# Hybrid encoder layer on one core: seven-product pairs with joined high and low activations, and products chained in a bank

## The reference

```python
xn = rmsnorm(h, g_pre_mix)
proj = xn @ w_in          # q, k, v of two attentions, and gate_a, gate_b
...
mix = (jax.nn.sigmoid(gate_a) * ya + jax.nn.sigmoid(gate_b) * yb) @ w_out
h = h + rmsnorm(mix, g_post_mix)
gu = rmsnorm(h, g_pre_ffn) @ w_ffn_in
g, u = jnp.split(gu, 2, axis=-1)
h = h + rmsnorm((jax.nn.silu(g) * u) @ w_ffn_out, g_post_ffn)
e = p_l @ w_ple
h = h + rmsnorm(jax.nn.sigmoid(h @ w_ple_gate) * e, g_ple)
```

## Time and profile before

| | |
|---|---|
| median of 3 runs | 2796.68 us (2796.5 to 2797.44) |
| profiled execution: span, first to last instruction | 2793.8 us |
| PE busy | 2759.9 us (99%) |
| PEld busy | 2465.9 us (88%) |
| DVE busy | 1677.4 us (60%) |
| ACT busy | 997.8 us (36%) |
| mean granted clock of TensorE | 0.998 |

### The profile page before, as it was taken

How to read it: one execution, slowest core, us unless ns; L and a number is a source line. 1 busy time by engine, 2 the same in 40 slices (tenths; PEclk the granted TensorE clock), 3 DMA queues, 4 the chain that set the end, 5 groups by cost and what they waited for, 6 DMA issues and landing times.

```text
span 2793.8 us, 41330 instructions
## 1 busy us (share of the span) xinstructions
PE 2759.9 (99%) x16624; PEld 2465.9 (88%) x16624; DVE 1677.4 (60%) x2113; ACT 997.8 (36%) x1323; POOL 18.3 (1%) x25
## 2 busy tenths in 40 slices
PE   8999999999999999999999999999999999999997
PEld 7999888888888888878999999999998888888886
DVE  7888555555554432376888888888883233234534
ACT  7333323323334322253444444444442121113422
POOL 0000000000000000000000000000000000000000
PEclk9999999999999999999999999999999999999999
DMA  6434422222225444253433333333327352443322
GB/s 251 151 114 136 138 76 75 75 84 83 75 91 163 138 153 141 91 196 136 151 114 141 122 132 131 125 138 117 146 92 295 103 181 99 157 155 124 131 96 105
DMA packets 158298, 364.75 MB, mean 131 GB/s; under 512 B 17142, under 2 KB 51438, under 8 KB 155630
## 3 DMA queue, kind: packets, MB, share of 16 engines
q1 hardware_dynamic: 146304, 325.33, 34.1%
q10 hardware_dynamic: 11886, 37.87, 3.4%
HBM read 321.15 MB, written 42.00 MB: 130 GB/s over the span
## 4 chain that ended last, share of the span: by engine, by line
PE 87%; issue 10%; DVE 1%; ACT 1%; DMA 1%; SPq 0%; POOL 0%; DVEq 0%; POOLq 0%
PE bank L2204 10%; PE bank L2202 10%; PE bank L2203 10%; PE bank L2122 10%; PE bank L2124 10%; PE bank L2123 10%; PE bank L1948 8%; PE bank L1946 8%; PE bank L1947 8%; PE bank L1979 1%; DMA x_f<-xT 0%; DVE resid_b L1643 0%; PE bank L2271 0%; PE bank L1967 0%; ACT x_f L771 0%
## 5 line engine op out<-in xcount | busy, mean ns | idle before, releaser
L736 ACT CAST w_hi<-w_raw 128x1024 fp32r<-128x1024 f32 x290 | 292.3, 1052 | 934.6 <-PE bank L2204 522.7
L1188 DVE TENSOR_TENSOR w_lo<-w_raw,w_hi 128x1024 fp32r<-128x1024 f32 x288 | 341.0, 1222 | 454.4 <-ACT w_hi L736 454.3
L2122 PE MATMUL bank<-act_hi,w_hi 128*128 128x256 f32 x1664 | 471.2, 283 | 2.4 <-DVE act_lo L1279 1.4
L2123 PE MATMUL bank<-act_lo,w_hi 128*128 128x256 f32 x1664 | 470.9, 283 | 0.0
L2124 PE MATMUL bank<-act_hi,w_lo 128*128 128x256 f32 x1664 | 470.9, 283 | 0.0
L2122 PEld LDWEIGHTS bank<-act_hi,w_hi 128*128 128x128 f32 x1664 | 319.4, 192 | 2.9 <-DVE act_lo L1279 1.6
L2123 PEld LDWEIGHTS bank<-act_lo,w_hi 128*128 128x128 f32 x1664 | 319.5, 192 | 0.1
L2124 PEld LDWEIGHTS bank<-act_hi,w_lo 128*128 128x128 f32 x1664 | 319.5, 192 | 0.0
L1946 PE MATMUL bank<-act_hi,w_hi 128*128 128x512 f32 x752 | 299.5, 398 | 1.2 <-DVE w_lo L1188 1.2
L1947 PE MATMUL bank<-act_lo,w_hi 128*128 128x512 f32 x752 | 293.2, 390 | 0.0
L1948 PE MATMUL bank<-act_hi,w_lo 128*128 128x512 f32 x752 | 293.1, 390 | 0.0
(11 more groups left out here) (263 smaller groups left out, 5422.5 us busy)
## 6 DMA issues: line engine op xcount, KB each, us to landing
w_raw<-w_in SPq DMA_DIRECT2D x92, 512.0 KB, 4.2
w_raw<-w_ffn_out SPq DMA_DIRECT2D x88, 512.0 KB, 4.5
w_a_even<-w_ffn_in SPq DMA_DIRECT2D x80, 512.0 KB, 5.3
w_a_odd<-w_ffn_in SPq DMA_DIRECT2D x60, 512.0 KB, 4.4
hid_dram<-hid_st ACTq DMA_DIRECT2D x44, 512.0 KB, 5.2
w_raw<-w_ffn_in SPq DMA_DIRECT2D x36, 512.0 KB, 5.4
w_raw<-w_out SPq DMA_DIRECT2D x32, 512.0 KB, 4.5
w_raw<-w_ple_gate SPq DMA_DIRECT2D x32, 512.0 KB, 4.3
```

The source lines that it names most:

```text
L736: nc.scalar.copy(w_hi[:, 2 * par + half], w_raw[:, half]).then_inc(hi_ready, 1)
L1188: nc.vector.tensor_tensor(w_lo[:, 2 * par + half], w_raw[:, half], w_hi[:, 2 * par + half].bitcast(F32), ALU.subtract).then_inc(lo_ready, 1)
L2122: nc.tensor.matmul(out, w_hi[:, slot, k], hi, start=k == 0, stop=False)
L2123: nc.tensor.matmul(out, w_hi[:, slot, k], lo, start=False, stop=False)
```

## The change

Each step k of a product has two matmuls in place of three: the high weights meet the high and the low activations side by side in one matmul of 512 columns, and the low weights meet the high activations in one of 256 columns, on the first half of the same bank. A bank then holds a product in its first half and a correction (high by low) in its second, and the two have to be added. Products that belong to one output are chained in one bank, each going on where the one before stopped: products 0 and 3 in bank a, 1 and 5 in bank g, 2, 4 and 6 in bank b, which starts from a copy of bank a after product 0. Two sets of three banks alternate from pair to pair. ACT copies a bank or half of one after products 0, 1, 2, 3, 4 and 6 (`keep_chain`), and DVE makes four sums into `gu` and `up` and two sums of 512 columns before them, in place of seven. In DVE's step for product j, `combine_first` stands ahead of `product_low` and `combine_second` behind it, and the multiplications L1813 and L1819 are behind them both. `act_hi` and `act_lo` become the two halves of one tensor.

```diff
@@ -130,7 +130,10 @@
 PRODUCT_FROM = ((0, 0), (1, None), (3, 0), (0, 1), (2, 2), (4, None), (0, 3))
 SUM_AT = {1: 1, 3: 2, 4: 3, 6: 4}
-LAST_READ = (1, 5, 1, 3, 4, 6, 7)
+CHAIN_BANKS = ((0, 1, 5), (2, 3, 4))
+CHAIN_OF = (0, 1, 2, 0, 2, 1, 2)
+COPIES = 6
+SUMS = 4
 def shape_constants():
...
@@ -175,8 +178,8 @@
-        act_hi = at("act_hi", R_X, [P, KT, T], F32R)
-        act_lo = at("act_lo", R_X + 32 * KB, [P, KT, T], F32R)
+        act_both = at("act_both", R_X, [P, 2, KT, T], F32R)
+        act_hi, act_lo = act_both[:, 0], act_both[:, 1]
...
@@ -235,10 +238,8 @@
-        x_sum = at("x_sum", R_Q + 54 * KB, [P, S])
-        y_sum = at("y_sum", R_Q + 55 * KB, [P, S])
-        v_sum = at("v_sum", R_Q + 48 * KB, [P, S])
-        first_product = at("first_product", R_Q + 49 * KB, [P, S])
+        second_kept = at("second_kept", R_Q + 48 * KB, [P, 2, S])
+        third_kept = at("third_kept", R_Q + 54 * KB, [P, 2, S])
...
@@ -271,6 +272,8 @@
+        fifth_kept = at("fifth_kept", R_S + 3 * KB, [P, 2, S])
+        low_half = at("low_half", R_S + 5 * KB, [P, 2, S])
...
@@ -817,6 +821,30 @@
+            def keep_chain(p, q, j, before):
+                a, g, b = CHAIN_BANKS[q % 2]
+                if j == 0:
+                    if before > 1:
+                        act.wait_ge(combined, p * SUMS - SUMS)
+                    nc.scalar.copy(bank[:, b], bank[:, a]).then_inc(kept, 1)
+                elif j == 1:
+                    if before:
+                        act.wait_ge(combined, p * SUMS - 2)
+                    nc.scalar.copy(second_kept[:].rearrange("p a t -> p (a t)"), bank[:, g]).then_inc(kept, 1)
+                elif j == 2:
+                    if before:
+                        act.wait_ge(combined, p * SUMS - 1)
+                    nc.scalar.copy(third_kept[:].rearrange("p a t -> p (a t)"), bank[:, b]).then_inc(kept, 1)
+                elif j == 3:
+                    nc.scalar.copy(low_half[:, 0], bank[:, a, S:]).then_inc(kept, 1)
+                elif j == 4:
+                    nc.scalar.copy(fifth_kept[:].rearrange("p a t -> p (a t)"), bank[:, b]).then_inc(kept, 1)
+                elif j == 6:
+                    if before:
+                        act.wait_ge(combined, p * SUMS)
+                    nc.scalar.copy(low_half[:, 1], bank[:, b, S:]).then_inc(kept, 1)
@@ -847,8 +875,9 @@
             for p in range(GATE_PAIRS):
                 for j in range(PRODUCTS):
                     act.wait_ge(op_done, p * PRODUCTS + j + 1)
-                    if j == 0:
-                        nc.scalar.copy(first_product[:], bank[:, 0, 0:S]).then_inc(first_kept, 1)
+                    if j == 0 and p < 2:
+                        act.wait_ge(unit_read, 3 + p)
+                    keep_chain(p, p, j, p)
                     p4, j4 = p + (j + 4) // PRODUCTS, (j + 4) % PRODUCTS
                     if p4 < GATE_PAIRS:
                         product_high(p4, p4 % 4, j4, H_GATES)
@@ -1106,8 +1135,7 @@
                     f = p0 + (CH + q)
                     for j in range(PRODUCTS):
                         act.wait_ge(op_done, p * PRODUCTS + (GATE_PAIRS * PRODUCTS + j + 1))
-                        if j == 0:
-                            nc.scalar.copy(first_product[:], bank[:, 0, 0:S]).then_inc(first_kept, 1)
+                        keep_chain(p0 + (GATE_PAIRS + q), q, j, GATE_PAIRS)
                         q4, j4 = q + (j + 4) // PRODUCTS, (j + 4) % PRODUCTS
                         if not (last and q4 == 4):
                             product_high(p0 + (GATE_PAIRS + q4), q4, j4, H_SEVEN)
...
@@ -1315,12 +1343,41 @@
-            def product(j):
-                return bank[:, j, 0:S]
-
+            def add_halves(dst, both):
+                return combine(dst, both[:, 0], both[:, 1])
+            def add_both(both, other):
+                return nc.vector.tensor_tensor(both[:].rearrange("p a t -> p (a t)"), both[:].rearrange("p a t -> p (a t)"),
+                                               other, ALU.add).then_inc(halves_added, 1)
+            def combine_first(p, q, j):
+                a, g, b = CHAIN_BANKS[q % 2]
+                if j == 3:
+                    dve.wait_ge(kept, p * COPIES + 4)
+                    combine(gu[:, 0], low_half[:, 0], bank[:, a, 0:S])
+                if j == 4:
+                    dve.wait_ge(kept, p * COPIES + 5)
+                    add_both(fifth_kept, second_kept[:].rearrange("p a t -> p (a t)"))
+                if j == 5:
+                    dve.wait_ge(op_done, p * PRODUCTS + 6)
+                    add_both(third_kept, bank[:, g])
+                if j == 6:
+                    dve.wait_ge(kept, p * COPIES + 6)
+                    combine(up[:, 0], low_half[:, 1], bank[:, b, 0:S])
+            def combine_second(p, j):
+                if j == 4:
+                    dve.wait_ge(halves_added, p * 2 + 1)
+                    add_halves(up[:, 1], fifth_kept)
+                if j == 5:
+                    dve.wait_ge(halves_added, p * 2 + 2)
+                    add_halves(gu[:, 1], third_kept)
...
@@ -1788,41 +1830,28 @@
                     p = p0 + q
                     f = p0 + (CH + q)
-                    def combined_before(i):
-                        dve.wait_ge(combined, p * PRODUCTS + (GATE_PAIRS * PRODUCTS + i))
-
+                    n = p0 + (GATE_PAIRS + q)
                     for j in range(PRODUCTS):
-                        if j >= 2:
-                            dve.wait_ge(op_done, p * PRODUCTS + (GATE_PAIRS * PRODUCTS + j + 1))
                         if j == 2:
-                            dve.wait_ge(first_kept, p + (GATE_PAIRS + 1))
-                            combine(x_sum[:], first_product[:], product(2))
-                            combined_before(1)
-                            combine(y_sum[:], x_sum[:], product(1))
+                            dve.wait_ge(op_done, n * PRODUCTS + (j + 1))
                         if j == 3:
                             dve.wait_ge(hid_lo_ready, f)
-                            combine(gu[:, 0], first_product[:], product(3))
-                        if j == 4:
-                            combine(v_sum[:], x_sum[:], product(4))
-                            combined_before(4)
-                            combine(up[:, 1], v_sum[:], product(1))
-                        if j == 5:
-                            combined_before(2)
-                            combine(gu[:, 1], y_sum[:], product(5))
-                            combined_before(6)
-                            nc.vector.tensor_tensor(gu[:].rearrange("p a t -> p (a t)"), gu[:].rearrange(
-                                "p a t -> p (a t)"), rstd[:], ALU.mult).then_inc(ffn_read, 1)
-                        if j == 6:
-                            combine(up[:, 0], v_sum[:], product(6))
-                            combined_before(7)
-                            dve.wait_ge(silu_ready, f + 1)
-                            nc.vector.scalar_tensor_tensor(gu[:], up[:], -1.0, gu[:], ALU.mult,
-                                                           ALU.mult).then_inc(hid_ready, 1)
+                        combine_first(n, q, j)
                         q4, j4 = q + (j + 4) // PRODUCTS, (j + 4) % PRODUCTS
                         if not (last and q4 == 4):
                             product_low(p0 + (GATE_PAIRS + q4), q4, j4, H_SEVEN)
                         else:
                             split_lo(N_FO + j4 // 2, (N_FO + j4 // 2) % 2, j4 % 2)
+                        combine_second(n, j)
+                        if j == 5:
+                            dve.wait_ge(combined, n * SUMS + 3)
+                            nc.vector.tensor_tensor(gu[:].rearrange("p a t -> p (a t)"), gu[:].rearrange(
+                                "p a t -> p (a t)"), rstd[:], ALU.mult).then_inc(ffn_read, 1)
+                        if j == 6:
+                            dve.wait_ge(combined, n * SUMS + 4)
+                            dve.wait_ge(silu_ready, f + 1)
+                            nc.vector.scalar_tensor_tensor(gu[:], up[:], -1.0, gu[:], ALU.mult,
+                                                           ALU.mult).then_inc(hid_ready, 1)
                         if first and q == 0 and j < 4:
                             d_low(12 + j)
                         if j == 1 and not (first and q == 0):
@@ -2107,32 +2136,44 @@
             def moving(j, k):
                 if j in (1, 2, 4):
-                    tile = {1: d1, 2: t2, 4: d2}[j]
-                    return tile[:, k, 0], tile[:, k, 1]
+                    return {1: d1, 2: t2, 4: d2}[j][:, k]
                 kk, ts = {0: (k, slice(0, S)), 3: (HALF + k, slice(0, S)), 5: (HALF + k, slice(S, T)),
                           6: (k, slice(S, T))}[j]
-                return act_hi[:, kk, ts], act_lo[:, kk, ts]
+                return act_both[:, :, kk, ts]
             def half_product(p, q, j, h):
                 pe.wait_ge(lo_ready, p * PRODUCTS + (h + j + 3))
```

(81 more changed lines are left out.)

17 lines of the change are left out of this document (1 added, 16 removed).

## The result

The changed kernel takes 2860.14 us (median of 4 runs, 2857.96 to 2861.06) against 2796.59 us before: a ratio of 1.0228, 95% interval 1.0214 to 1.0241. It is 63.5 us slower. The forecast was slower, at 2834 us, with a range up to 2855 us: the direction was right, and the time lies outside the range.

What follows compares the result with a forecast made beforehand. PE was taken to set the pace, DVE close behind. FFN loop + 43.3, first FFN pair - 0.7, gates - 8.9 gave + 33.7 us; with span-to-median 2.9 and 3.9 for L1819, 2834 us, range 2795 to 2855.

Steps and rivals of the forecast that it cites:

- PE set the pace before, and DVE and ACT had room as work: FFN pairs: PE busy all of 808.00 us; after the change DVE's work 16.95 and ACT's 11.0 us of 19.42.
- The loop: FFN pairs: ring through silu, hidden tile and bank copy takes 21.27 us against 20.16 now, + 43.3 us; chance 0.72.
- 0.1 for L1819: FFN pairs: L1819 waits for two semaphores and starts 0.1 us later, 3.9 us in all.
- The linear sum: PE's products: one matmul dropped per step saves 0.0132 us, 0.742 us a pair, 38.6 us over 52 pairs.
- the halves' distance: Joined matmul's halves lie 32 KB apart, unseen in any row; bounds were the linear sum and no gain, 0.360 a step.
- The 2.5 ns a matmul: PE: by the skill's issue gap, 56 dropped matmuls would be worth 0.14 us a pair, not 0.74.
- There PE's gain stands: Gate pairs: ACT's copy is hidden, so 12 pairs gain 0.742 us each, - 8.9 us.
- PE keeps the pace everywhere: Rival: ACT's copy of bank a ends within 5.4 us of the pair's start; 2758 us, chance 0.13 with partial gains.
- the two cancel: Rival: a loop of 20.3 to 20.55 us in the FFN pairs gives 2791 to 2802 us; chance 0.07.
- Joining: Rival: joining the matmuls gains PE nothing, products stay at 2.88 us; 2852 us, chance 0.06.
- The clock: Rival: PE's clock falls in the new gaps, products 2 and 3 at 1.2 GHz; some 3050 us, chance 0.02.

Runs made afterwards that it cites:

- e1: Changed kernel with both second sums and both multiplications (L1848, L1853) put ahead of the low parts in DVE's FFN step: 2782.98 us, ratio 0.9957 to the kernel before.
- e4: Changed kernel without the two 512-column additions of each pair, so one summand of two outputs is missing: 2864.58 us, ratio 1.0245 to the kernel before.
- e2: Changed kernel with ACT's copy of bank a put ahead of the hidden tile's high part of the pair before: 2808.12 us, ratio 1.0047 to the kernel before.
- e9: Changed kernel with only the third sum and L1848 put ahead of the low part in step 5: 2787.67 us, ratio 0.9966 to the kernel before.
- e10: Changed kernel with only L1853 put ahead of the low part in step 6: 2794.28 us, ratio 0.9994 to the kernel before.
- e6: Kernel before with only the joined 512-column and the 256-column matmul per step, no chain, copies or added sums: 2776.71 us, ratio 0.9930.
- e8: e7 with one weight tile fetched on SP ahead of the sixteen table transfers behind the gates: 2768.41 us, ratio 0.9899 to the kernel before.
- e3: Changed kernel with e1's order in the last FFN pair only: 2847.14 us, ratio 1.0191 to the kernel before.
- e7: e1 with each product's eight 512-column matmuls first, then its eight 256-column ones: 2775.33 us, ratio 0.9925 to the kernel before.

## Why the prediction was wrong, point by point

- **PE set the pace before, and DVE and ACT had room as work.** Right: with e1's order the same work fits in 19.80 us a pair, and 1.2 us less work (e4) gains nothing.
- **The loop.** Right in mechanism, place and size. Forecast 21.27 us (and 0.1 for L1819), measured 21.44 and 21.53. In the round shown the copy starts within 0.02 us of the forecast, PE starts 0.09 us late, and the other 0.08 us are products 2 and 3 at PE's slower pace. The gap is ahead of product 2, released by ACT's copy, 39 times. The FFN pairs cost 49.3 us where 43.3 - 0.7 + 3.9 = 46.5 were forecast. e2, e9 and e10 each cut the loop at another link, e1 at two.
- **PE's gain.** The linear sum, 0.0132 us a step and 0.742 us a pair, was reached in e1's gate pairs. In the changed kernel's gate pairs, and in the FFN pairs of e1 and e6, PE had its slow pace: 0.0066 us a step, 20.16 - 19.79 = 0.37 us a pair, and e6 shows this half by itself (19.4 of 38.6 us). So the term was mis-sized by half for the run that it was to forecast. I had bounded the unknown by the halves' distance, which costs nothing (e6); two paces of the same matmuls were not in the list. The 2.5 ns a matmul of the Trainium skill (TensorE: Matmul & The Clock Gate, Back-to-back issue gap), named in the prediction, would have been worth 0.14 us a pair, against 0.37 at the slow pace.
- **The gates: "There PE's gain stands".** This step failed. Forecast were - 8.9 us for the gate pairs and nothing behind them; the first FFN product came 3.2 us late: 12.1 us apart. Of these, 6.7 lie in the gate pairs, which gave 2.25 us and not 8.9: 4.5 by the slow pace (12 pairs at 0.37 us), and the rest by a wait of 3.9 us in the first pair, where two of 1.0 and 1.4 stood before, and a lower clock behind it (0.90 from 68 to 74 us). 5.4 lie behind them. I followed ACT's copies and DVE in the gates, and not what comes behind them on SP: a tile queued behind sixteen table transfers. PE arrived earlier, stood 3.65 us (before: 1.23), and started at a lower clock. e8 shows that 5.0 us come back when the tile is fetched first. SP goes on to these transfers only behind `pair_out`, DVE's last multiplication of the gate pairs, and that ended at 304.26 us (before: 304.05), though PE was 2.25 us ahead; in both traces ACT waits there for tiles of `w_in` (2.86 and 3.29 us the longest wait). What would bring this date forward no run shows.
- **The end of the FFN stage.** It had no term at all; with the gates, this is what put the time out of the range. I priced the moved sums by what DVE does in a usual pair. In the last one the low part that they were moved behind is of the output weights, which a transfer brings late, and PE's next stage waits for the third sum. 9.8 us of wait and 1.9 us of restart at 0.53 of the clock; e3 takes 6.8 us off the wait and 1.6 us off what comes behind it.

The account closes: forecast + 33.7 + 3.9 = 37.6 us; + 2.8 for the pairs, + 12.1 for the gates and behind them, + 11.7 for the end is 64.2 us, the difference of the spans. That the loop's own term came out so near is no luck, as its steps agree one by one; but of the terms beside it one was half right and one missing, and both erred the same way.

- **The rivals.** That PE keeps the pace everywhere (2758 us) failed, as does "the two cancel". Joining did gain, but half. The clock did not fall in the 39 gaps of 1.3 to 1.7 us: it was 1.00 over the FFN pairs. This rival was nearer than its chance says: in e4, with gaps longer by up to 0.2 us, it fell three times.

What stays open: why grouped 512-column matmuls of this kernel start 0.230 us apart where the earlier trace rows show 0.2268, what chooses between the two paces of the alternating ones, and why PE waits 3.9 us in the first gate pair.

## What to carry to other kernels

When an operation is moved on one engine, follow every result that stood ahead of it round to where it comes back: here DVE's two multiplications, moved behind 1.1 us of work each, made a ring through ACT and PE that no busy share shows, and a cut at one link of it was worth 52 us (e2) to 72 us (e9). Then do the same for the first and the last round of the loop, where the operation next to it is another one, with another thing to wait for. A gain on the engine that sets the pace is only kept if the next stage's data come earlier too. And before an edit is credited with a difference of some microseconds, the landmarks ahead of it should be compared: here the same code ahead of the edit differed by 5 to 6 us from one trace to another.

## What the runs showed of the hardware

- Matmuls of 512 and 256 columns in turn start 0.230 and 0.117 us apart in some stretches and 0.237 and 0.117 in others, in the same code at a granted clock of 1.00 (gate pairs of e1 and of the changed kernel); grouped by eight, 0.230 and 0.120 (e7). So one dropped 256-column matmul in three gave 13.3 ns at the fast pace and 6.6 at the slow one.
- ACT's copy of 512 columns from PSUM to PSUM took 0.58 us, as one to SBUF.
- Thirty-nine gaps of 1.3 to 1.7 us, one in every 21.5 us, left the granted clock at 1.00; in e4, with gaps of 1.4 to 1.9 us, it fell behind three of them (1.87, 1.81 and 1.75 us), to 0.79 over 8 us, and not behind others of 1.77 us. A gap of 9.64 us was followed by matmuls at a granted clock of 0.53, that is near 1.2 GHz, for about 3 us, and one of 3.65 us by a stretch at 0.78; yet in e3 a wait of 3.6 us at the same place was followed by a clock of 1.00.
